# Feed-forward tiles of a streaming-encoder trunk: one half of the columns after the other, instead of both in turn

## The reference, cut to what matters

```python
def rmsnorm(x, gain):
    y = x * lax.rsqrt(jnp.mean(x * x, axis=-1, keepdims=True) + EPS)
    return y * gain

def swiglu(x, w_gate, w_up, w_down):
    return (jax.nn.silu(x @ w_gate) * (x @ w_up)) @ w_down

for layer in range(2):
    h = h + 0.5 * swiglu(rmsnorm(h, norm_ff1[layer]), ...)   # feed-forward 0, then 2
    hn = rmsnorm(h, norm_mix[layer])
    # layer 0: gated convolution beside a complex diagonal state space model
    # layer 1: sliding-window attention; the 16 learned tokens are dropped from h behind it
    h = h + mixer(hn)
    h = h + 0.5 * swiglu(rmsnorm(h, norm_ff2[layer]), ...)   # feed-forward 1, then 3
```

## Time and profile before

| | |
|---|---|
| median of 3 runs | 1878.01 us (1877.99 to 1879.36) |
| profiled execution | 1878.34 us |
| its span | 1876.5 us, mean granted TensorE clock 0.999 |
| TensorE, matmul records | 1867.1 us busy, 99% of the span, 13919 |
| TensorE, weight loads | 1767.1 us, 94%, 13919 |
| VectorE | 959.9 us, 51% |
| ScalarE | 598.4 us, 32% |
| GpSimd | 350.1 us, 19% |
| chain that ended last | TensorE 96% of the span; line 807, the helper's matmul, 79% |

### The profile page before, as it was taken

One profiled execution on the slowest core, in us unless ns is written; L12 is line 12 of the kernel. 1 busy time (PEld: TensorE's weight loads), 2 busy tenths in 40 slices (PEclk: granted clock), 3 DMA queues, 4 the chain that ended last, 5 costly groups with the idle time before them and its releaser, 6 DMA issues.

```text
span 1876.5 us, 33932 instructions
## 1 busy us (share of the span) xinstructions
PE 1867.1 (99%) x13919; PEld 1767.1 (94%) x13919; DVE 959.9 (51%) x1083; ACT 598.4 (32%) x702; POOL 350.1 (19%) x629
## 2 busy tenths in 40 slices
PE   9999999999999999999999999999999999999999
PEld 8999999999999999999999999999988788888887
DVE  6443356668865443344564443445557654434443
ACT  5222222332243222222342222223456442222232
POOL 2888889315230000000000000000012000000000
PEclk9999999999999999999999999999999999999999
DMA  6322544447423332332243223322321233333322
GB/s 184 90 84 84 155 135 130 162 140 191 118 73 89 94 89 86 110 90 73 71 126 90 84 84 101 90 81 80 115 62 46 66 93 94 90 96 101 111 70 87
DMA packets 330785, 188.29 MB, mean 100 GB/s; under 512 B 8152, under 2 KB 323832, under 8 KB 330712
## 3 DMA queue, kind: packets, MB, share of 16 engines
q1 hardware_dynamic: 323216, 166.71, 30.0%
q0 software_dynamic: 7088, 20.38, 3.9%
q10 hardware_dynamic: 408, 0.17, 0.0%
HBM read 174.91 MB, written 11.14 MB: 99 GB/s over the span
## 4 chain that ended last, share of the span: by engine, by line
PE 96%; DVE 2%; issue 1%; ACT 1%; POOL 0%; POOLq 0%; DVEq 0%
PE ps L807 79%; PE ps L1048 5%; PE ps L1159 2%; PE ps L1090 2%; PE ps L1109 1%; PE ps L1298 1%; PE ps L1260 1%; PE ps L1200 0%; PE ps L1009 0%; PE ps L1008 0%; PE ps L999 0%; DVE r L1621 0%; PE ps L1221 0%; PE ps L1211 0%; ACT xh L1321 0%
## 5 line engine op out<-in xcount | busy, mean ns | idle before, releaser
L807 PE MATMUL ps<-xh,wh 128*128 128x264 f32 (+1 forms) x2432 | 557.7, 299 | 0.3 <-DVE t_a L1653 0.2
L807 PE MATMUL ps<-xh,wl 128*128 128x264 f32 (+1 forms) x2432 | 556.6, 299 | 0.0
L807 PE MATMUL ps<-xl,wh 128*128 128x264 f32 (+1 forms) x2432 | 556.6, 299 | 0.0
L1591 DVE TENSOR_TENSOR wl<-raw,wh 128x2048 fp32r<-128x2048 f32 x171 | 400.2, 2340 | 168.4 <-ACT wh L1309 168.4
L1309 ACT ACTIVATE wh<-raw 128x2048 fp32r<-128x2048 f32 x172 | 327.6, 1905 | 246.4 <-PE ps L807 205.5
L807 PEld LDWEIGHTS ps<-xh,wh 128*128 128x128 f32 x2432 | 385.4, 188 | 15.1 <-issue 1.5
L807 PEld LDWEIGHTS ps<-xl,wh 128*128 128x128 f32 x2432 | 385.2, 188 | 13.8 <-issue 0.2
L807 PEld LDWEIGHTS ps<-xh,wl 128*128 128x128 f32 x2432 | 385.2, 188 | 13.8
L807 PE MATMUL ps<-act_h,wh 128*128 128x264 f32 (+1 forms) x1232 | 282.2, 299 | 0.0
L807 PE MATMUL ps<-act_h,wl 128*128 128x264 f32 (+1 forms) x1232 | 281.7, 299 | 0.0
L807 PE MATMUL ps<-act_l,wh 128*128 128x264 f32 (+1 forms) x1232 | 281.6, 298 | 0.0
(11 more groups left out here) (313 smaller groups left out, 1685.9 us busy)
## 6 DMA issues: line engine op xcount, KB each, us to landing
raw<-in_ff_w_gate SPq DMA_DIRECT2D x88, 512.0 KB, 3.7
raw<-in_ff_w_up SPq DMA_DIRECT2D x87, 512.0 KB, 4.7
raw<-in_ff_w_down SPq DMA_DIRECT2D x64, 384.0 KB, 3.8
raw<-in_ff_w_down SPq DMA_DIRECT2D x64, 320.0 KB, 3.5
raw<-in_even_w_in SPq DMA_DIRECT2D x16, 512.0 KB, 4.8
raw<-in_attn_w_qkv SPq DMA_DIRECT2D x12, 512.0 KB, 4.5
raw<-in_even_w_out SPq DMA_DIRECT2D x8, 512.0 KB, 4.3
raw<-in_attn_w_o SPq DMA_DIRECT2D x8, 512.0 KB, 4.4
```

Of the source, the lines that this page charges most:

```text
L807: last = nc.tensor.matmul(ps[:, 2 * pair + hf, 0:nh], w[:, slot, b * P:(b + 1) * P], x[:, k0 + k, c0 + hf * nh:c0 + (hf + 1) * nh], start= ...
L1591: v.tensor_tensor(wl[:, c % 2, :], raw[:, c % 2, :], wh[:, c % 2, :].bitcast(F32), ALU.subtract).then_inc(wl_ready, 1)
```

## The change

The loop over the two halves of the columns is taken from the innermost place in `mm3` to the outermost. A tile now runs all contraction blocks and all three products for columns 0 to 263 into its first bank, then all of them for columns 264 to 527 into its second. The wait `before_last` is made once, in the first half. Where a tile has one half (feed-forward 3) nothing changes.

```diff
--- before.py
+++ after.py
@@ -799,11 +799,11 @@
 
                 c0, nh, nb = col
                 n = len(blocks)
-                for k, b in enumerate(blocks):
-                    if k == n - n_last and before_last:
-                        before_last()
-                    for q, (w, x) in enumerate(((wh, x_h), (wh, x_l), (wl, x_h))):
-                        for hf in range(nb):
+                for hf in range(nb):
+                    for k, b in enumerate(blocks):
+                        if k == n - n_last and before_last and hf == 0:
+                            before_last()
+                        for q, (w, x) in enumerate(((wh, x_h), (wh, x_l), (wl, x_h))):
                             last = nc.tensor.matmul(ps[:, 2 * pair + hf, 0:nh], w[:, slot, b * P:(b + 1) * P],
                                                     x[:, k0 + k, c0 + hf * nh:c0 + (hf + 1) * nh],
                                                     start=(k == 0 and q == 0), stop=(k == n - 1 and q == 2))
```

## The result

The changed kernel takes 1892.72 us (median of 3 runs, 1892.28 to 1893.01), the kernel before 1878.01 us. The ratio is 1.0076, with a 95% interval from 1.0059 to 1.0093: 0.8% slower, where 0.17% was forecast. The prediction was wrong: the time lies beyond its range (1878.3 to 1885.0), and it gave "slower" 0.38, of which 0.09 for the mechanism that came.

What follows compares the result with a forecast made beforehand. TensorE, over 99% busy, bounds the kernel; rate change 0 plus norm waits 2.24 and 10-block down waits 0.99 us make 3.2 us, so 1881.2 us by the median (0.17% slower), range 1878.3 to 1885.0.

Steps and rivals of the forecast that it cites:

- What bounds the kernel: Whole kernel: TensorE has matmul records over 99% of the span, so no idle share that a new order could fill.
- The waits: First tiles after a norm and down tiles: TensorE waits earlier for its last contraction block, adding 3.2 us together.
- The 12-block tiles: Three down tiles of 12 blocks: the operand comes in time by 0.58 us, so they add 0.
- The extra 0.16 us of a real wait: At each new TensorE wait: 0.16 us beyond the lateness, since the weight load can't run ahead; ends 0 and 0.22.
- the two norm waits: First norm tiles of feed-forwards 1 and 2: operand 0.96 us late, plus 0.16 each, 2.24 us together.
- The rate: The helper's 9408 matmuls of 264 columns: step stays 120.0 ns in the new order, change 0.
- The forecast's own sign against its first part: In the profile after: a step other than 120.0 ns, or displacement growing evenly along a feed-forward, refutes the unchanged rate.
- dearer matmuls: Rival, the helper's 264-wide matmuls: fresh weights into the predecessor's bank cost 3.6 ns each, 33.9 us, 1912; chance 0.09.
- cheaper matmuls: Rival, the helper's 264-wide matmuls: no switching between banks saves 3.0 ns each, 28 us, giving 1853; chance 0.08.
- The waits bit in full: Answers the rival that new TensorE waits bite less or not: 1880.3 in part, 1878.0 in full; chance 0.08.
- The clock didn't fall in the new pauses: Answers the rival that each norm pause lowers the granted clock, 1.7 us apiece, 6.6 in all, 1884.6; chance 0.05.
- The rule on weights: Trainium skill's rule for TensorE: one load serves many matmuls, so the new order would add loads; forecast rejected it.

Runs made afterwards that it cites:

- early_wait: Kernel before, matmul order untouched, with only the wait for the last block made as early as in the changed kernel: 1882.74 us, ratio 1.0016.
- turns: Whole computation left out: loops of 96 264-wide matmuls varying how often halves alternate and what lies between; 120.0 ns alternating every matmul, 121.7 after 2 and 3.
- steps: Whole computation left out: loops of 96 matmuls varying order, first column, bank, width and weights; from column 264 alone 122.1 to 122.2 ns in either bank.
- starts: Whole computation left out: loops of 96 matmuls varying first column, width and weight columns; 128 to 240 columns step by 111 to 113 ns.

## Why the prediction was wrong, point by point

- **What bounds the kernel**: right. TensorE was busy in every slot, so each nanosecond of a step and each wait came through in full.
- **The waits**: right, in place, number and size. Forecast 2 x 1.12 + 3 x 0.33 = 3.2 us; in the trace 1.12, 1.07 and 3 x 0.33, and early_wait gave 3.0 us (1.3 to 4.7) with the waits alone. The 12-block tiles didn't wait. The extra 0.16 us of a real wait, read from the earlier trace rows, held. In the list of waits the two norm waits stand with 0.85 and 0.81 us, below the 0.9 to 1.1 that the forecast looked for there, since that list leaves out what the start of the next matmul shows. Not foreseen was the late weight tile, 0.7 us.
- **The rate**: this step failed. "I take a change of the rate of 0" had to be 1.10 ns, 10.3 us, three quarters of the loss. Its reasons were not good enough. Equal distances in the earlier trace rows say what a right half costs behind a left one, not behind a right one: exactly what the change takes away. By themselves, right halves step by 122.2 ns and left ones by 120.0 or 121.4; in turn they take 120.0. The 0.11 us of the earlier trace rows was at 128 columns, with weights only 66 columns wide; from 128 to 240 the step hardly depends on the width, and narrower weights alone took away the price of column 264, so that this row bounds nothing at 264. The 512-wide row doesn't speak of right halves either: those matmuls all start at one column. It was also not true that each matmul takes fresh weights in the new order: high x high and low x high share theirs. The forecast's own sign against its first part did show: a displacement that grows along a feed-forward and not in jumps. Feed-forward 1 begins at 581.28 instead of 577.25, 4.0 us later, where 0.3 was forecast.
- **The rival "dearer matmuls"** is what happened, with a third of its price: 1.1 ns of the 3.6. The forecast had the point from which it decides, 0.4 ns, and 0.09 for its chance. Its 1912 leaves out the 3.2 us of the waits, which its 1853 for cheaper matmuls takes in; with them it would be 1915. Its two mechanisms are refuted, though: neither fresh weights (L104 of turns) nor the same bank (L84 and L86, and L104, of steps) cost anything by itself. What it read rightly is that matmuls in a row don't all carry the same time beside their stream, and that the old order stood at the low end, 10.0 ns. A trace with 10.0 and 13.6 should have been given more than one chance in eleven.
- **The other rivals**: cheaper matmuls did not come. The waits bit in full. The clock didn't fall in the new pauses: the granted clock was 1.00 in 583 to 586 and in 970 to 973, and the one low stretch before, 0.57 at 1379, came again as 0.59 at 1393. The pause at 536 that this rival went by was 0.29 us of idle time and not half a microsecond.
- **The rule on weights**: the loads are 13919 before and after. One set of weights for two matmuls in a row saved nothing in either kernel.

What stays open is why. Shown is that the step of 264-wide matmuls depends on the sequence of their first columns and on what ran before, that neither the bank, nor fresh weights, nor the other engines are needed for it, and that it lies between 120.0 and 123.4 ns. The weight loads as such are not ruled out: with 64 weight columns the price of column 264 was gone. Why both halves are slow in the 10-block down tiles, and by which part of the chip all this comes about, no run tells. No kernel was found that beats the one before.

## What to carry to other kernels

When TensorE has no idle time, the step between matmuls is the figure to guard: 1 ns in 120 was 10 us here, and neither the busy share nor any list of waits shows it. Divide a long piece of the chain by its count before and after every change of order. A step read from one order vouches for that order alone, and a loop of 96 matmuls in the new order would have warned of this change: turns after 24 gave 120.9 against 120.0 ns, 0.9 of the 1.1. Such a loop needs company, though, since one and the same loop gave 120.0 or 121.4 from column 0, and 120.0 or 123.4 from column 32, by what ran before it.

## What the runs showed of the hardware

- In the loops by themselves, matmuls of 128 to 240 columns with 128 weight columns step by 111 to 113 ns, 256 by 116.8 to 120.0, 264 by 120.0 to 123.4, 272 by 125.3 to 125.7 (L120 and L122 of steps), 512 by 226.8 to 233.3 (L126 of steps, L132 of starts).
- A moving operand that begins 8 columns further right costs a 512-wide matmul 6.6 ns (233.5 to 226.9), over all of feed-forward 3's 1356 in the chain 9 us.
- Two starts that alternate can be faster than either repeated: from 0 and 264 the pair takes 240.0 ns, where matmuls from 264 alone take 244.4.
- With 64 weight columns instead of 128, 264-wide matmuls from column 264 alone step by 120.0 ns (L146 of starts) instead of 122.2.
